# Reading moving tiles and writing banks from the last column to the first in a three-product float32 matmul

## The chip, the core and the metric

One Trainium2 chip, of which the kernel uses one core. TensorE multiplies a stationary tile of 128 x 128 by a moving tile of 128 partitions and up to 512 columns, and writes the output into one of eight banks of 512 float32 columns per partition. VectorE (DVE), ScalarE (ACT) and GpSimd (POOL) do the work between products; SyncE (SP) and GpSimd issue the transfers. The metric is the device time in microseconds of one execution; lower is better. The kernel before takes 2105.55 us, the median of 2 runs (2105.32 to 2105.77).

## The reference

One layer of a hybrid network over 512 latent tokens and 256 context tokens of 2048 features, all in float32:

- Modulation: `silu(cond) @ w_ada + b_ada` gives shifts, scales and gates, for the latent condition `c` and for the context condition `c_ctx`.
- Mixer: the normalised, modulated tokens go through `w_in` (2048 x 3072). A third is a Fourier part (a 2-D transform over tokens and 256 channels in each of four groups, then `w_fourier`), a third is the input of a recurrent part (a convolution of 4 taps, gates in 8 heads of 128, one scan forward and one backward, both seeded with the states of the context tokens), a third is its gelu gate. The two results are concatenated and go through `w_out` (2048 x 2048). The result is normalised, gated and added to `x`.
- Feed-forward: the normalised, modulated `x` goes through `w_up` (2048 x 11264), a convolution of 3 taps over tokens, `gelu(g) * v`, and `w_down` (5632 x 2048), and is again normalised, gated and added.

The output is the latent stream, 512 x 2048.

## The kernel before, in words

**Layout.** Features lie on the partitions, tokens on the columns: a tile of 128 features has 512 latent columns (`L`) or 256 context columns (`C`), so a token order is a column order. The 16 tiles of the normalised input are `h_hi` and `h_lo` (`hc_hi` and `hc_lo` for the context).

**Products of three.** Each float32 operand is split into a high part rounded to the format float32r (`_hi`, written by ScalarE) and the rest (`_lo`, written by VectorE as the difference). A product of two such operands is the sum of three float32r matmuls into the same bank: high by high, high weight by low moving tile, low weight by high moving tile. The helper `three` on TensorE issues them (lines 988, 989, 990), so nearly all matmuls of the kernel carry one of these three line numbers, whatever their stage. `start` clears the bank's sum at the first product, `stop` ends it at the last.

**Stages.** First the squares of `x` and of the context are summed over features by products with a matrix of ones (lines 998, 1001, 1027; the context's squares are written to `csq0` and half of `sq0`, two squares of 256 columns in each, by ScalarE at line 635). Then eight rounds of modulation: TensorE multiplies the two condition columns by strips of `w_ada` (line 1013), ScalarE copies the resulting rows from a bank to `ada_rows` (line 651, `copy_rows`), and TensorE turns them into columns by small products (line 1022, `turn`); the first input projections run between these rounds. Then come the other heads' projections and gates, the Fourier part, the output projection, and the feed-forward part in 11 chunks of 4 pairs of tiles. In each pair a part of the contraction is done by `seven_products`, with halves of 256 columns (`H`) in place of 512; `down` follows for the chunk before. The last chunk is finished in halves of 256 columns, and the residual is added at the end.

**Order of work.** Each engine has its own program, written out by hand. Weights come as a stream of units of 128 x 1024 float32 (512 KB), loaded by SP into a ring of slots (`w_raw`), rounded by ScalarE (line 602, `w_hi`) and split by VectorE (line 1532, `w_lo`). TensorE waits for `lo_done` once per unit, and its last product of a unit or of a bank raises the semaphore for whoever reads the bank or refills the slot. Banks are reused in turns.

**Plain products.** Sums over features or tokens use unsplit float32 operands; the compiler issues each as two instructions with the same columns. Line 1486 adds the residual this way through a moving tile made of two pieces of 256 columns (`x1_two`); lines 1468 to 1474 sum squares of 256 columns.

**Buffers.** `sq0`, `csq0`, `ss_x`, `ss_c`, `pos0`, `ada_rows` and the ring `ada0_raw` for the strips of `w_ada` stand one behind the other in a region that later stages use for other tiles.

**Falling column order before.** VectorE already walks some tiles from the last column to the first: the backward scans of the recurrent part (lines 1688 and 1691, beside the forward one in line 1685), the folding of tokens `n` and `512 - n` in the Fourier part (lines 1725 and 1726), and its unfolding (line 1771, whose sources are a tile and a bank, beside line 1769, which reads them forward).

Of the kernel before, what the change touches and what calls it, by code (L numbers as in the profile page):

```python
# [10 lines left out]
ACT = mybir.ActivationFunctionType  # L11
ds = bass.ds

P = 128
# [151 lines left out]
def build(nc, x1_d, x_t, ctx_t, par_d, late_d, stream, ada0, adabg, gates_d, tabs_d, wf_d, out_t):  # L166
    ctx = ExitStack()
    with ctx:
        def sem(name):
            return ctx.enter_context(nc.semaphore(name))  # L170

        def sbuf(stack, name, shape, dt=F32, side=None):
            return stack.enter_context(nc.sbuf_tensor(name, shape, dt, side=side))

        def twice(stack, raw, name, shape):

            with ExitStack() as s:
                first = sbuf(s, raw, shape)
            return first, sbuf(stack, name, shape, F32R)
# [34 lines left out]
        with ExitStack() as s:  # L214
            c0, hc_lo = twice(s, "c0", "hc_lo", [P, KT, C])
            hc_hi = sbuf(s, "hc_hi", [P, KT, C], F32R)
            with ExitStack() as s0:
                sq0 = sbuf(s0, "sq0", [P, 2, L])
                csq0 = sbuf(s0, "csq0", [P, 2, C])
                ss_x = sbuf(s0, "ss_x", [P, L])  # L220
                ss_c = sbuf(s0, "ss_c", [P, C])
                pos0 = sbuf(s0, "pos0", [P, NPOS])
                ada_rows = sbuf(s0, "ada_rows", [P, 2 * P])
                ada0_raw = sbuf(s0, "ada0_raw", [P, A0SLOTS, 1024])

        ada_raw12 = sbuf(mixer, "ada_raw12", [P, 2, ACOL], side="right")
# [137 lines left out]
        def rows_bank(c):  # L364

            return bank[5 + 2 * (c % 2)]
# [12 lines left out]
        a0_used, rows_copied, turned, mod_made = sem("a0_used"), sem("rows_copied"), sem("turned"), sem("mod_made")  # L379
# [209 lines left out]
        def _(act):  # L589
            chain = Chain(act, act_chain)  # L590
            a = nc.scalar
# [55 lines left out]
            def copy_rows(c):  # L647
                act.wait_ge(a0_used, A0UNITS * (c + 1))
                if c > 0:
                    act.wait_ge(turned, c)  # L650
                a.activation(ada_rows[:, :], rows_bank(c)[:, 0:2 * P], ACT.Copy).then_inc(rows_copied, 1)

            def round_h(c):
                for k in range(2 * c, 2 * c + 2):
# [6 lines left out]
            for c in range(NADA):  # L661
                copy_rows(c)
                round_h(c)
                hi(c + 1)
# [290 lines left out]
            c = NCH - 1  # L955
# [27 lines left out]
        def _(pe):  # L983
            t = nc.tensor

            def three(out, w, w_l, v, v_l, start, stop):

                t.matmul(out, w, v, start=start, stop=False)  # L988
                t.matmul(out, w, v_l, start=False, stop=False)  # L989
                return t.matmul(out, w_l, v, start=False, stop=stop)  # L990
# [54 lines left out]
            def gates_of_two(k):  # L1045

                for h in range(2):
                    mm = three(bank[UG_BANK[h]][:, :], *block_of(k // 2, 2 * h + k % 2), h_hi[:, k, :], h_lo[:, k, :],
                               k == 0, k == KT - 1)
                    if k == KT - 1:  # L1050
                        mm.then_inc(first_ug, 1)

            def inputs_of_two(k):

                for h in range(2):
                    bx, bc = ux_bank(h)
                    w, w_l = block_of(k // 2, 4 + 2 * h + k % 2)
                    three(bx[:, :], w, w_l, h_hi[:, k, :], h_lo[:, k, :], k == 0, k == KT - 1)
                    mm = three(bc[:, 0:C], w, w_l, hc_hi[:, k, :], hc_lo[:, k, :], k == 0, k == KT - 1)
                if k % 2:  # L1060
                    mm.then_inc(unit_used, 1)
# [381 lines left out]
            c = NCH - 1  # L1443
# [871 lines left out]
```

## Time and profile before

| | |
|---|---|
| Median of 2 runs | 2105.55 us |
| The profiled execution | 2105.41 us |
| Its span, first to last instruction | 2103.6 us |
| TensorE matmuls | 2071.2 us busy, 11682 instructions |
| TensorE weight loads | 1772.5 us |
| VectorE | 1529.6 us |
| ScalarE | 811.6 us |
| GpSimd | 78.7 us |
| DMA | 311.19 MB, mean 148 GB/s |
| Mean granted clock of TensorE | 0.996 |

Busy time is the time in which an engine has at least one instruction under way. Matmuls overlap in the pipeline: the duration of one is longer than the distance from its start to the next one's, so the pace of a series is read from the starts. `PE` is TensorE's matmuls, `PEld` its weight loads.

### The profile page before, as it was taken

Reading aid. Unit: us, or ns where it says so; the run is one execution under the profiler, and the core shown is the slowest. Engines: PE = TensorE matmul, PEld = TensorE weight load, DVE = VectorE, ACT = ScalarE, POOL = GpSimd, SP = SyncE. Lnnn points to the kernel's source line nnn. Section 1 sums busy time; section 2 is a strip of 40 time slices with the busy share of each in tenths; the row PEclk is TensorE's granted clock in tenths of the full one; section 3 lists DMA queues with packets and bytes.
Section 4 is the critical chain, followed back from the end, with each engine's and each line's share of the span. In section 5 each row is a group of like instructions: output and inputs, shape, how many; then the busy total and the mean of one; then the engine's idle time right before and its main releaser. Section 6 shows DMA issues by size and latency. Waiting matters only on the chain.

```text
span 2103.6 us, 28297 instructions
## 1 busy us (share of the span) xinstructions
PE 2071.2 (98%) x11682; PEld 1772.5 (84%) x11682; DVE 1529.6 (73%) x2202; ACT 811.6 (39%) x1077; POOL 78.7 (4%) x145
## 2 busy tenths in 40 slices
PE   7999999999999999999999999999999999999998
PEld 4678887888777888888889898898988889888887
DVE  5567978876988975867767676676766758577577
ACT  5346577543323442423324233332333424233243
POOL 0000000001110000000000000000000000000002
PEclk9999999999999999999999999999999999999999
DMA  9953424434876523333333333334233333232343
GB/s 394 408 204 110 154 96 161 137 109 173 323 277 225 181 90 134 100 128 111 110 130 101 138 103 103 129 101 140 100 120 121 100 130 100 91 101 101 100 172 109
DMA packets 86193, 311.19 MB, mean 148 GB/s; under 512 B 9456, under 2 KB 13552, under 8 KB 84016
## 3 DMA queue, kind: packets, MB, share of 16 engines
q1 hardware_dynamic: 67824, 243.09, 32.7%
q0 software_dynamic: 17424, 65.50, 9.1%
q8 instruction: 92, 1.51, 0.3%
q10 hardware_dynamic: 816, 0.79, 0.1%
q14 instruction: 37, 0.30, 0.0%
HBM read 300.95 MB, written 8.39 MB: 147 GB/s over the span
## 4 chain that ended last, share of the span: by engine, by line
PE 80%; DVE 2%; ACT 1%; DMA 1%; issue 0%; DVEq 0%; ACTq 0%
PE bank L988 26%; PE bank L990 26%; PE bank L989 26%; DMA w_raw<-in_stream 1%; PE bank L1099 1%; DVE acc L2167 0%; PE bank L1284 0%; DVE w_lo L1532 0%; ACT w_hi L602 0%; PE bank L1313 0%; PE bank L1194 0%; DVE acc L2139 0%; ACT lru_u L698 0%; DVE cv L1544 0%; DVE x L2193 0%
## 5 line engine op out<-in xcount | busy, mean ns | idle before, releaser
L988 PE MATMUL bank<-h_hi,w_hi 128*128 128x512 f32 (+1 forms) x1968 | 711.2, 361 | 4.2 <-ACT y_lru L671 1.2
L989 PE MATMUL bank<-h_lo,w_hi 128*128 128x512 f32 (+1 forms) x1968 | 708.6, 360 | 0.0
L990 PE MATMUL bank<-h_hi,w_lo 128*128 128x512 f32 (+1 forms) x1968 | 707.2, 359 | 0.0
L1532 DVE TENSOR_TENSOR w_lo<-w_raw,w_hi 128x1024 fp32r<-128x1024 f32 x260 | 316.0, 1222 | 157.9 <-ACT w_hi L602 157.8
L988 PEld LDWEIGHTS bank<-h_hi,w_hi 128*128 128x128 f32 x1968 | 372.3, 189 | 63.6 <-issue 11.9
L602 ACT ACTIVATE w_hi<-w_raw 128x1024 fp32r<-128x1024 f32 x260 | 273.0, 1056 | 389.1 <-DMA w_raw<-in_stream 389.0
L990 PEld LDWEIGHTS bank<-h_hi,w_lo 128*128 128x128 f32 x1968 | 372.1, 189 | 56.6
L989 PEld LDWEIGHTS bank<-h_lo,w_hi 128*128 128x128 f32 x1968 | 372.3, 189 | 49.0
L988 PE MATMUL bank<-act_hi,w_hi 128*128 128x512 f32 (+1 forms) x688 | 265.0, 385 | 1.7 <-DVE acc L2139 1.5
L990 PE MATMUL bank<-act_hi,w_lo 128*128 128x512 f32 (+1 forms) x688 | 264.2, 384 | 0.0
L989 PE MATMUL bank<-act_lo,w_hi 128*128 128x512 f32 (+1 forms) x688 | 264.2, 384 | 0.0
L598 ACT ACTIVATE w_hi<-w_raw 128x1024 fp32r<-128x1024 f32 x80 | 84.9, 1062 | 339.4 <-DVE w_raw L2040 339.4
L2067 DVE TENSOR_TENSOR acc<-acc,bank 128x512 f32<-128x512 f32 x144 | 98.3, 686 | 136.9 <-PE bank L990 136.9
L988 PEld LDWEIGHTS bank<-act_hi,w_hi 128*128 128x128 f32 x688 | 129.2, 188 | 27.9 <-DVE h_lo L1532 1.9
L989 PEld LDWEIGHTS bank<-act_lo,w_hi 128*128 128x128 f32 x688 | 129.3, 188 | 25.7
L990 PEld LDWEIGHTS bank<-act_hi,w_lo 128*128 128x128 f32 x688 | 129.3, 188 | 25.6
L1564 DVE SCALAR_TENSOR_TENSOR ada_acc<-ada_raw,csil,ada_acc 128x1024 f32<-128x1024 f32 x105 | 134.5, 1281 | 10.9 <-DMA ada_raw<-in_adabg 6.7
L550 POOL DMA_DIRECT2D ada_raw<-in_adabg x112 | 59.5, 532 | 1538.6 <-DVE ada_acc L1564 1139.1
L1528 DVE TENSOR_TENSOR w_lo<-w_raw,w_hi 128x1024 fp32r<-128x1024 f32 x80 | 97.5, 1219 | 0.0
L988 PE MATMUL bank<-t_hi,w_hi 128*128 128x256 f32 x320 | 90.6, 283 | 0.0
L989 PE MATMUL bank<-t_lo,w_hi 128*128 128x256 f32 x320 | 90.6, 283 | 0.0
L990 PE MATMUL bank<-t_hi,w_lo 128*128 128x256 f32 x320 | 90.5, 283 | 0.0
(340 smaller groups left out, 2711.4 us busy)
## 6 DMA issues: line engine op xcount, KB each, us to landing
w_raw<-in_stream SPq DMA_DIRECT2D x340, 512.0 KB, 3.5
ada_raw<-in_adabg POOLq DMA_DIRECT2D x112, 512.0 KB, 4.3
ada_raw<-in_ada SPq DMA_DIRECT2D x64, 512.0 KB, 13.5
x<-in_x_t SPq DMA_DIRECT2D x4, 1024.0 KB, 8.4
acc<-in_adabg SPq DMA_DIRECT2D x8, 512.0 KB, 6.1
x<-in_x_t POOLq DMA_DIRECT2D x4, 1024.0 KB, 9.4
x_kept_d<-x SPq DMA_DIRECT2D x4, 1024.0 KB, 5.6
c<-in_ctx_t SPq DMA_DIRECT2D x2, 1024.0 KB, 14.3
```

Of the source, the lines that this page charges most:

```text
L550: pool.dma_start(ada_raw(slot), adabg[COLS[q // KT] * KT + q % KT]).then_inc(ada_in[slot], 16)
L598: a.activation(hi_unit(n), raw_unit(n), ACT.Copy)
L602: a.activation(hi_unit(n), raw_unit(n), ACT.Copy).then_inc(hi_done, 1)
L988: t.matmul(out, w, v, start=start, stop=False)
L989: t.matmul(out, w, v_l, start=False, stop=False)
L990: return t.matmul(out, w_l, v, start=False, stop=stop)
L1099: mm = t.matmul(b[:, at + j:at + j + 1], ada_acc(n)[:, P * j:P * j + P], ones[:, 0:1], start=True, stop=True)
L1528: v.tensor_tensor(lo_unit(n), raw_unit(n), hi_unit(n).bitcast(F32), ALU.subtract)
L1532: v.tensor_tensor(lo_unit(n), raw_unit(n), hi_unit(n).bitcast(F32), ALU.subtract).then_inc(lo_done, 1)
L1564: v.scalar_tensor_tensor(dst, ada_raw(s), scale, dst, ALU.mult, ALU.add).then_inc(ada_eaten, 1)
L2067: v.tensor_tensor(tile(acc, m), tile(acc, m), bank[4 + m % 4][:, :], ALU.add).then_inc(down_added, 1)
```

## The change

The first thing in `three` is now to reverse the column order of its output and of both moving tiles. All three products thus read the moving tile from its last column to its first and write the output's columns from the last to the first; the weights stay as they are, and column j of the moving tile still goes to column j of the output. Products that do not go through `three` are untouched. Besides, `ada_rows` has no place of its own any more, and is the first half of `csq0`.

```diff
@@ -220,7 +220,7 @@
                 ss_x = sbuf(s0, "ss_x", [P, L])
                 ss_c = sbuf(s0, "ss_c", [P, C])
                 pos0 = sbuf(s0, "pos0", [P, NPOS])
-                ada_rows = sbuf(s0, "ada_rows", [P, 2 * P])
+                ada_rows = csq0[:, 0, :]
                 ada0_raw = sbuf(s0, "ada0_raw", [P, A0SLOTS, 1024])
@@ -648,7 +648,7 @@
                 act.wait_ge(a0_used, A0UNITS * (c + 1))
                 if c > 0:
                     act.wait_ge(turned, c)
-                a.activation(ada_rows[:, :], rows_bank(c)[:, 0:2 * P], ACT.Copy).then_inc(rows_copied, 1)
+                a.activation(ada_rows, rows_bank(c)[:, 0:2 * P], ACT.Copy).then_inc(rows_copied, 1)
@@ -985,6 +985,7 @@
             def three(out, w, w_l, v, v_l, start, stop):
 
+                out, v, v_l = out[:, ::-1], v[:, ::-1], v_l[:, ::-1]
                 t.matmul(out, w, v, start=start, stop=False)
                 t.matmul(out, w, v_l, start=False, stop=False)
                 return t.matmul(out, w_l, v, start=False, stop=stop)
```

## Rows read from the trace of the kernel before

**Rows 1.** The page: busy time, and TensorE's rows of 40 slices.

```profile
PE 2071.2 (98%) x11682; PEld 1772.5 (84%) x11682; DVE 1529.6 (73%) x2202; ACT 811.6 (39%) x1077; POOL 78.7 (4%) x145
...
PE   7999999999999999999999999999999999999998
...
PEclk9999999999999999999999999999999999999999
```

**Rows 2.** The page: the chain that ended last, by line.

```profile
PE bank L988 26%; PE bank L990 26%; PE bank L989 26%; DMA w_raw<-in_stream 1%; PE bank L1099 1%; DVE acc L2167 0%; PE bank L1284 0%; DVE w_lo L1532 0%; ACT w_hi L602 0%; PE bank L1313 0%; PE bank L1194 0%; DVE acc L2139 0%; ACT lru_u L698 0%; DVE cv L1544 0%; DVE x L2193 0%
```

**Rows 3.** Windows: busy time of each engine, clock, from 684 to 1500 us.

```profile
684.00:1500.00 816.00, 816.00 (x4520) 715.28 (x4519) 587.82 (x836) 281.29 (x342) 12.68 (x24) 1.00 0.35 119
```

**Rows 4.** Groups of line 988 by form: count, busy us, mean ns of one.

```profile
L988 PE MATMUL bank<-h_hi,w_hi 128*128 128x512 f32 x1408 | 552.9, 393 | 4.2 <-ACT y_lru L671 1.2 <-DVE hc_lo L1618 0.8 <-ACT sq L607 0.7
...
L988 PE MATMUL bank<-act_hi,w_hi 128*128 128x512 f32 x656 | 255.5, 390 | 0.1
...
L988 PE MATMUL bank<-h_hi,w_hi 128*128 128x256 f32 x560 | 158.3, 283 | 0.0
L988 PE MATMUL bank<-t_hi,w_hi 128*128 128x256 f32 x320 | 90.6, 283 | 0.0
...
L988 PE MATMUL bank<-t_hi,sums_hi 128*128 128x256 f32 x160 | 45.4, 284 | 0.0
...
L988 PE MATMUL bank<-hc_hi,w_hi 128*128 128x256 f32 x128 | 35.7, 279 | 0.0
...
L988 PE MATMUL bank<-h_hi,sums_hi 128*128 128x256 f32 x80 | 22.4, 280 | 0.0
...
L988 PE MATMUL bank<-act_hi,h_hi 128*128 128x256 f32 x64 | 18.2, 284 | 0.4 <-DVE acc L2139 0.4
...
L988 PE MATMUL bank<-xc_hi,g_hi 128*128 128x512 f32 x32 | 12.8, 400 | 3.5 <-issue 3.5
...
L988 PE MATMUL bank<-xc_hi,g_hi 128*128 128x256 f32 x32 | 9.0, 280 | 0.0
```

**Rows 5.** Timeline of TensorE: start us, us of one; a series' first and the next's.

```profile
1500.18 0.39 PE L988 MATMUL bank<-h_hi,w_hi 128*128 128x512 f32 x1
...
1509.70 0.28 PE L988 MATMUL bank<-h_hi,w_hi 128*128 128x256 f32 x1
...
1519.74 0.39 PE L988 MATMUL bank<-h_hi,w_hi 128*128 128x512 f32 x1
```

**Rows 6.** Timeline of TensorE: plain float32 products near the end.

```profile
2085.84 1.02 PE L1486 MATMUL bank<-late_raw,par 128*128 128x512 f32 x2
2086.69 0.59 PE L1468 MATMUL bank<-up_sum,par 128*128 128x256 f32 x2
2087.12 0.59 PE L1469 MATMUL bank<-up_sum,par 128*128 128x256 f32 x2
```

**Rows 7.** Groups of VectorE by form: forward and backward over columns.

```profile
L2036 DVE TENSOR_TENSOR sums_raw<-w_raw 128x256 f32<-128x256 f32 x40 | 16.7, 418 | 0.0
...
L1685 DVE TENSOR_TENSOR_SCAN lru_u<-lru_r,lru_i 128x768 f32<-128x768 f32 x8 | 14.1, 1758 | 0.3
...
L1691 DVE TENSOR_TENSOR_SCAN lru_u<-lru_r,lru_u,lru_i 128x512 f32<-128x512 f32 x8 | 10.3, 1285 | 0.3
...
L1688 DVE TENSOR_TENSOR_SCAN lru_u<-lru_r,lru_i 128x256 f32<-128x256 f32 x8 | 5.5, 691 | 0.3
...
L1769 DVE TENSOR_TENSOR y_four<-eo,bank 128x256 f32<-128x256 f32 x8 | 3.4, 422 | 0.3
...
L1726 DVE TENSOR_TENSOR eo<-y_four 128x255 f32<-128x255 f32 x8 | 3.3, 417 | 0.0
L1771 DVE TENSOR_TENSOR y_four<-eo,bank 128x255 f32<-128x255 f32 x8 | 3.3, 411 | 0.0
```

**Rows 8.** Timeline of ScalarE around the first copy of the rows.

```profile
29.38 0.85 ACT L635 ACTIVATE csq<-c 128x256 f32<-128x256 f32 x2 [0.91 <-PE bank L1027]
...
36.62 0.38 ACT L651 ACTIVATE ada_rows<-bank 128x256 f32<-128x256 f32 x1 [1.31 <-PE bank L1013]
```

## The prediction

> **What bounds the kernel now.** I read the page first, then the chain, then the groups, then single instructions. The busy table gives TensorE 2071.2 us of a span of 2103.6, and its row of forty slices stands at 9 but for the first and last; the granted clock is 9 or more tenths throughout, the higher of the two levels (2.4 GHz) [rows 1]. The chain of waits puts 26% of the span on each of lines 988, 989 and 990, the three products of `three`, and all else below 2% a line [rows 2]. In the long middle (684 to 1500 us) TensorE is busy 816.00 of 816.00 us while VectorE, next in line, has 587.82 [rows 3]. So nothing but TensorE sets the time there, and what happens to one product of `three` reaches the end almost undiminished.
>
> The size of that lever comes from counting. The groups by form [rows 4] show line 988 with 1408 + 656 + 32 = 2096 products of 512 columns and 560 + 320 + 160 + 128 + 80 + 64 + 5 x 32 = 1472 of 256 (32 of these 258); lines 989 and 990 repeat each count. That is 6288 long and 4416 short products. Their durations (393 and 283 ns) overlap, so the pace has to be read from start to start: 42 long ones from 1500.18 to 1509.70 us, 0.2267 us each; 84 short ones from 1509.70 to 1519.74, 0.1195 us each [rows 5]. 6288 x 0.2267 = 1425 us and 4416 x 0.1195 = 528 us: **1953 us**, 93% of the span, runs through the edited line. Doubling 256 columns adds 0.1072 us, 0.419 ns a column; what is left, 0.1195 - 0.1072 = 0.012 us, is a fixed part per product.
>
> **The change part by part.** *(a) The direction.* No instruction is added or removed: 10,704 products keep weights, sizes, order, bank and start and stop flags. Column j of the moving tile still goes to column j of the output, so only the order in time inside one product changes, and the finished bank is signalled by the same last product. No semaphore, DMA or queue moves; VectorE, ScalarE, SP and GpSimd see the same events. The only unknown is the price of a column when both address streams step by minus one element.
>
> No row of before has TensorE stepping backward, so I bound it. Above: the trace has the engine at a slower rate per column in its plain float32 instructions, 0.425 us for 512 columns (two instructions in 0.85 us, 2085.84 to 2086.69) and 0.215 for 256 (two in 0.43 us, 2086.69 to 2087.12) [rows 6]. At that rate the products cost 6288 x (0.425 - 0.2267) + 4416 x (0.215 - 0.1195) = 1247 + 422 = +1669 us. With the fixed 0.012 us kept on top of a doubled column price the additions are 0.2144 and 0.1072 us: 1348 + 473 = +1821 us. Below: at most the fixed part could vanish, 10,704 x 0.012 = -131 us.
>
> Between these ends I take 0, by the rows nearest in kind. VectorE already does this exact access elsewhere: line 1771 reads `cosine[:, C-1:0:-1]` in SBUF and `b[:, C-1:0:-1]` in a bank backward, 411 ns for 255 columns, beside 422 for 256 forward in line 1769; line 1726, one source of which runs backward in SBUF, takes 417 ns for 255, beside 418 for 256 forward in line 2036 [rows 7]. The memories thus give float32 columns in falling order at the same rate to that engine. Against leaning on it: VectorE takes one column in over 1 ns, TensorE in 0.42, so a path of its own that handles neighbours together could still trip. The reversed scans are mildly worrying: from 256 to 512 columns they add 1285 - 691 = 594 ns, 2.32 a column, where the whole forward scan of 768 takes 1758, 2.29 with its fixed part [rows 7]; at most some per cent. A gap in the moving tile is no burden either: line 1486 reads two separate runs of 256 at the 0.425 us that go into the slower rate above, but that rate may hide it [rows 6].
>
> The bank is where I see the risk. The Trainium skill ("PSUM — Partial Sum Buffer", Specifications) says that the bank's lines are 8 bytes, two float32 values, and that any non-contiguous pattern slows matmuls significantly. No row here shows TensorE writing a bank so. If a step of minus one counts as non-contiguous, the sum is the upper one above; if only leaving a line counts, falling pairs share lines as rising ones do, and the sum is 0.
>
> *(b) The shared buffer.* ScalarE's eight copies of 383 ns (line 651) now land in `csq0`'s first half. Its last squares are written by 29.38 + 0.85 = 30.23 us and summed before ScalarE can pass its wait for all 16 sums ahead of line 610; the first copy starts at 36.62, after an idle 1.31 us for TensorE's line 1013 [rows 8]. Program order already enforces this, no wait is added, and the 32 small products of line 1022 read 256 contiguous columns as before. The tile frees 1 KB per partition and moves only `ada0_raw`, whose 64 loads keep their waits. Cost 0; both ends: below 0 there is no wait to remove, above, even one copy fully exposed each time would be 8 x 0.383 = 3.1 us.
>
> **Sum.** 2105.41 (this profiled execution; 1.8 us outside its span) + 0 + 0 = 2105.4, and the median of the runs shown is 2105.55: **2105.5 us**, own range 2100 to 2112.
>
> **The rivals.**
> *Half rate (slower).* Place: every product of `three`, at the bank's write or the moving tile's read, where two neighbouring columns are taken together only when the address rises. It decides as soon as a column costs more than it does now: 2% of the time, 42 us, is 3.9 ns a product. Price +1669 to +1821 us: 3774 to 3926 us. For it: a column at 0.42 ns is faster than any other engine's, and 93% of the span has no slack [rows 3, 5]. Against it: rows 7. Chance 26%.
> *A turn at each product (slower).* The pipeline from one product into the next works only forward, and the fixed part doubles: +131 us, 2236 us. Forward, too, each product jumps back to the column where the one before began, and reversing keeps a jump of that length, which speaks against it. 6%. Slower than all these, with reading and writing each tripping: 3%.
> *The fixed part shrinks (faster).* If the 12 ns per product belong to the direction, up to -131 us, 1974 us. Plain instructions have only 2 x 0.215 - 0.425 = 0.005 us of it [rows 6], so it is not the engine's floor; but they repeat the same weights more often, which explains it better. 6%.
> *The edit does nothing:* the reversal of both sides could be folded away before the chip, with the same time; it lies inside the first case.
>
> **How the numbers follow.** No change 59%, half rate 26%, a turn 6%, beyond 3%, faster 6%. A measurement here tells about 2%, 42 us, from no change. Faster by over 2%: 0.06; within: 0.59; slower: 0.35. With no change alone at 59%, the range must take in the half rate too: 2100 to 3930 us, leaving out the faster case and the one beyond.
>
> **What would show it.** Right: long products start every 0.227 us and short ones every 0.120, 26% of the chain on each of the three lines, line 651 with the same 383 ns and waits. Half rate: 0.42 to 0.44 and 0.21 to 0.23 us, VectorE's busy share near 40% instead of 73%, ScalarE waiting on TensorE. A turn: both sizes later by the same ns, instead of in proportion to columns. The forecast fails if TensorE or its bank port takes falling addresses singly; the shared buffer fails if line 651 or 1022 shows a new releaser.

## The result: 1.6% slower, and the profile after

The changed kernel takes 2138.44 us (two runs, 2137.11 and 2139.77) against 2105.55 before: ratio 1.0156, 95% interval 1.0113 to 1.0200. That is 33 us more where the forecast had none, far from the 1670 to 1820 us of the half rate. It lies between the likeliest case's own range (to 2112 us) and the rivals, inside the wide range only because that reached to the half rate.

The page of the kernel after: busy times, TensorE's slices and granted clock, and the chain by line (the three products are now lines 989, 990 and 991).

```profile
PE 2108.4 (99%) x11682; PEld 1772.4 (83%) x11682; DVE 1530.2 (72%) x2202; ACT 810.9 (38%) x1077; POOL 78.6 (4%) x145
...
PE   7999999999999999999999999999999999999998
...
PEclk9999999999999999999999999999999999999999
...
PE bank L989 27%; PE bank L990 27%; PE bank L991 27%; DMA w_raw<-in_stream 1%; PE bank L1100 1%; DVE acc L2168 0%; PE bank L1309 0%; PE bank L1285 0%; PE bank L1195 0%; ACT w_hi L602 0%; DVE w_lo L1533 0%; PE bank L1314 0%; DVE acc L2140 0%; DVE cv L1545 0%; ACT lru_u L698 0%
```

Against [rows 1] TensorE gained 37.2 us of busy time with the same number of instructions; weight loads, VectorE, ScalarE and GpSimd moved by less than 1 us, and the clock still stands in the nines. The chain is the one of [rows 2]. The window of [rows 3], after:

```profile
684.00:1500.00 816.00, 815.46 (x4432) 698.40 (x4431) 578.95 (x823) 274.95 (x335) 12.68 (x24) 1.00 0.36 116
```

In the same 816 us TensorE gets through 4432 products where it did 4520, and waits for only half a microsecond (815.46 of 816.00 busy): 1.9% fewer in a stretch whose granted clock is 1.00 before and after. So each product got dearer. The timeline of TensorE after, where a series of long products and one of short ones begin (compare [rows 5]):

```profile
1525.15 0.40 PE L989 MATMUL bank<-h_hi,w_hi 128*128 128x512 f32 x1
...
1536.35 0.28 PE L989 MATMUL bank<-h_hi,w_hi 128*128 128x256 f32 x1
...
1546.28 0.40 PE L989 MATMUL bank<-h_hi,w_hi 128*128 128x512 f32 x1
```

48 long products in 11.20 us are 0.2333 us each (0.2267 before), 84 short ones in 9.93 us are 0.1182 (0.1195). The long ones lost 6.6 ns and the short ones gained 1.3. 6288 x 6.6 - 4416 x 1.3 = 41.5 - 5.7 = +35.8 us, where the two spans differ by 34.4: the paces of these two series explain the result within 1.4 us, and no wait does. They are a little larger than the average. Over all starts of the two traces, gaps of 300 ns and more left out, a long product goes from 227.4 to 233.4 ns and a short one from 120.6 to 119.5: 6288 x 6.0 - 4416 x 1.1 = 37.7 - 4.9 = +32.8 us.

The shared buffer did what was said of it. ScalarE's copies after, against [rows 8]:

```profile
L651 ACT ACTIVATE csq<-bank x8: 383/383/383, 36.9 to 117.8; 128x256 f32<-128x256 f32 x8
```

### The profile page after: what moved, and what is told of

Its sections match the earlier page's. It is cut to its first block, busy times and chain, and to the rows that moved or that the text cites. A ratio compares the mean times of both kernels' runs of the same rounds, so it can differ in the third digit from the quotient of the medians.

```text
span 2138.0 us, 28297 instructions
## 1 busy us (share of the span) xinstructions
PE 2108.4 (99%) x11682; PEld 1772.4 (83%) x11682; DVE 1530.2 (72%) x2202; ACT 810.9 (38%) x1077; POOL 78.6 (4%) x145
## 4 chain that ended last, share of the span: by engine, by line
PE 81%; DVE 1%; ACT 1%; DMA 1%; issue 0%; DVEq 0%
PE bank L989 27%; PE bank L990 27%; PE bank L991 27%; DMA w_raw<-in_stream 1%; PE bank L1100 1%; DVE acc L2168 0%; PE bank L1309 0%; PE bank L1285 0%; PE bank L1195 0%; ACT w_hi L602 0%; DVE w_lo L1533 0%; PE bank L1314 0%; DVE acc L2140 0%; DVE cv L1545 0%; ACT lru_u L698 0%
## 5 line engine op out<-in xcount | busy, mean ns | idle before, releaser
L989 PE MATMUL bank<-h_hi,w_hi 128*128 128x512 f32 (+1 forms) x1968 | 720.8, 366 | 3.0 <-ACT y_lru L671 1.1
L990 PE MATMUL bank<-h_lo,w_hi 128*128 128x512 f32 (+1 forms) x1968 | 719.4, 366 | 0.0
L991 PE MATMUL bank<-h_hi,w_lo 128*128 128x512 f32 (+1 forms) x1968 | 717.5, 365 | 0.0
L989 PE MATMUL bank<-act_hi,w_hi 128*128 128x512 f32 (+1 forms) x688 | 270.4, 393 | 1.5 <-DVE acc L2140 1.5
L991 PE MATMUL bank<-act_hi,w_lo 128*128 128x512 f32 (+1 forms) x688 | 269.7, 392 | 0.0
L990 PE MATMUL bank<-act_lo,w_hi 128*128 128x512 f32 (+1 forms) x688 | 269.7, 392 | 0.0
```

## The experiments

Theories at the start: the price sits in TensorE's read of the moving tile; in its write of the bank; in the shared buffer; or in traffic from other engines. Paces below are start to start of a whole series, divided by its count. In the separate kernels one row of the timeline is one series.

### e2, e3: the two edits apart

e2 adds only the reversal line to the kernel before; e3 changes only the buffer (and the copy in line 651 that writes it, left out here):

```diff
-                ada_rows = sbuf(s0, "ada_rows", [P, 2 * P])
+                ada_rows = csq0[:, 0, :]
```

> Only the reversal in the three products, the buffer of the rows left as before. The direction carries all: ratio 1.0156 to 1.0165, near 2139 us, long products every 0.233 us, short ones every 0.118. The shared buffer carries some: visibly less, below 1.010.

> Only the shared buffer, products forward. Theory of a free buffer: 1.000 within 0.002, 2105.5 us, line 651 at 383 ns with the same releaser. Rival, a cost by placement or order: anything over 1.002, up to the 33 us of the whole change.

Measured: e2 2137.25 us, ratio 1.0149 (1.0135 to 1.0163); e3 2106.71 us, ratio 1.0002 (0.9992 to 1.0013), line 651 at 383 ns. The direction carries all of it (a little less than the 1.0156 that I had expected at least), the buffer nothing that can be measured.

### e6, e7: reading backward and writing backward apart

```diff
+                v, v_l = v[:, ::-1], v_l[:, ::-1]        # e6
+                out = out[:, ::-1]                       # e7, instead
```

> Only the moving tiles are read backward, the output is written forward, so tokens come out in reverse order and the result is not the reference's; buffer as before. From the separate kernel (233.3 ns with read back at either direction of the write): the whole loss is here, ratio 1.014 to 1.017, long products 0.233 us. Rival, the write shares the loss inside the whole kernel: ratio below 1.010.

> Only the output is written backward, moving tiles are read forward; tokens come out in reverse order, so the result is not the reference's; buffer as before. From the separate kernel (227.5 ns against 226.7): no loss, ratio 0.998 to 1.003, long products 0.227 us, short ones 0.1195. The rival of the prediction's risk at the bank: up to 1.015.

Measured: e6 2137.26 us, ratio 1.0148 (1.0133 to 1.0164); e7 2106.00 us, ratio 0.9998 (0.9989 to 1.0008). The timeline of e7 keeps the paces of before, 48 long products in 10.90 us (0.2271) and 84 short ones in 10.04 us (0.1195):

```profile
1520.44 0.39 PE L989 MATMUL bank<-h_hi,w_hi 128*128 128x512 f32 x1
...
1531.34 0.28 PE L989 MATMUL bank<-h_hi,w_hi 128*128 128x256 f32 x1
...
1541.38 0.39 PE L989 MATMUL bank<-h_hi,w_hi 128*128 128x512 f32 x1
```

The bank, which I had called the risk, takes falling columns for nothing that can be measured: reading backward alone costs what the whole reversal costs, writing backward alone nothing. All of the loss is in the read.

### e4, e8: short and long products apart

```diff
+                if out.shape[-1] < L:                    # e4; e8: == L
+                    out, v, v_l = out[:, ::-1], v[:, ::-1], v_l[:, ::-1]
```

> Only products of fewer than 512 columns are reversed (4416 of 10704), buffer as before. By the paces of the two traces these gain some 1.0 to 1.2 ns each: 4.4 to 5.3 us faster, ratio 0.9975 to 0.9979, and the loss of the whole change sits in the 6288 long ones (6.6 ns each, 41.5 us). Rival: the reversal costs something at every product and the short ones' nearer starts are given back in waits: 1.000 or above.

> Only the 6288 products of 512 columns are reversed, both sides, buffer as before. Sum of the whole change less what the short ones gave: 1.0149 + 0.0031 = 1.018, 2144 us; long products 0.233 us, short ones 0.1195. Rival, the parts do not add (the gain of the short ones came only with less time elsewhere): 1.015 or below.

Measured: e4 2099.32 us, ratio 0.9969 (0.9956 to 0.9981), faster than the kernel before; e8 2148.21 us, ratio 1.0197 (1.0182 to 1.0212). e8's excess of 42 us is near the 6288 x 6.6 ns = 41.5 of its term; e4's gain of 7 us is a little above the 5.7 of its own and the 5.3 that I had expected at most. e8's ratio lies just above its expected 1.018, which had been made from e2's 1.0149 and e4's measured gain of 0.0031; the 0.0017 between is within what the three intervals leave open. Both signs are clear of the noise, and the whole change is their difference.

### e1, e5: TensorE alone

No edit: separate kernels that load once, then issue series of products like this one.

```python
for i in range(24):  # 512 read back, write back
    mm = t.matmul(bank[2][0:128, 511::-1], w[:, 128 * (i % 16):128 * (i % 16) + 128], v[:, i % 4, 511::-1], ...)
```

> A separate kernel that computes none of the reference: after one load it issues series of 24 products (float32r unless said), TensorE alone at work, with moving tile and output each forward or backward, 512, 384, 256 or 128 columns, and some with narrower or repeated weights. Theory P (the price is one per column, on TensorE itself): a backward product costs 0.4557 ns a column and no fixed part, a forward one 0.4167 a column and 13.3 ns; so 512: 226.7 forward, 233.3 backward; 384: 173.3 and 175.0; 256: 120.0 and 116.7; 128: both held at 112 to 120 by the weight load. Theory F (a fixed price of a long product, as a boundary that only 512 columns cross): 384 backward 160 to 166 or 180, not 175. Rival O (other engines' traffic makes the difference in the whole kernel): alone, backward and forward are equal within 1 ns at every size. Theory R (the moving tile's read): read back, write forward has the backward pace. Theory W (the bank's write): read forward, write back has it. If the weight load disturbs the read, weights of 32 columns bring forward and backward together near 216 ns.

The timeline of e1: start, time of the series, line. Lines 65, 67, 69, 71 are 512 columns with read and write forward; both backward; read backward only; write backward only. Lines 81, 83 are 256 columns forward and both backward. Lines 113, 115 are the same at 512 columns in bfloat16.

```profile
28.51 5.60 PE L65 MATMUL bank<-v,w 128*128 128x512 f32 x24
33.95 5.77 PE L67 MATMUL bank<-v,w 128*128 128x512 f32 x24
39.55 5.76 PE L69 MATMUL bank<-v,w 128*128 128x512 f32 x24
45.15 5.62 PE L71 MATMUL bank<-v,w 128*128 128x512 f32 x24
50.61 4.35 PE L73 MATMUL bank<-v,w 128*128 128x384 f32 x24
...
67.49 3.03 PE L81 MATMUL bank<-v,w 128*128 128x256 f32 x24
70.36 3.01 PE L83 MATMUL bank<-v,w 128*128 128x256 f32 x24
73.20 3.00 PE L85 MATMUL bank<-v,w 128*128 128x256 f32 x24
...
133.94 5.36 PE L113 MATMUL bank<-vb,wb 128*128 128x512 bf16 x24
139.13 5.34 PE L115 MATMUL bank<-vb,wb 128*128 128x512 bf16 x24
144.31 5.34 PE L117 MATMUL bank<-vb,wb 128*128 128x512 bf16 x24
```

From each start to the next, over 24: 226.7, 233.3, 233.3 and 227.5 ns at 512 columns; 119.6 and 118.3 at 256; 216 and 216 in bfloat16. The effect is whole with TensorE alone, so rival O (other engines) falls, theory R stands and W falls. bfloat16 has neither the loss nor the extra 11 ns that even the forward float32r product carries. Theory P had 512 right, whose paces it was made from, and 384 forward nearly (174.2); backward, 384 columns took 177.9 ns, between P's 175.0 and F's 180, and neither came. Weights of 32 columns gave 229.6 forward and 233.3 backward, not 216: a shorter weight load does not remove the loss. It takes nearly half of the forward advantage away instead, for which e9 offers a possible reason below.

> The second separate kernel, none of the reference: series of 24 float32r products, TensorE alone, of 64 to 512 columns forward and backward with weights of 32 columns (so that the weight load limits nothing) and of 192 to 480 with weights of 128; then 512 columns in other orders: the two halves swapped but forward within; groups of eight and of four, last group first, forward within; groups of four and of 32 in rising order, backward within; halves backward within; even then odd columns; 256 columns from column 2, 4 and 8; 512 with another bank each time. Theory G (the loss grows with the length of an unbroken falling run): 227 forward and 233 backward at 512, crossing near 300 columns, and halves backward within near twice the 118 ns of 256 columns (237) or, if the run and not the instruction counts, below 233. Theory L (a lost step at every line or group boundary crossed downward): groups of four, last first, cost as much as backward (233) or more, and groups backward within but rising cost no more than forward (227). Rival (a fixed price of a falling start address at the next product's beginning): all patterns that begin at the last column cost 233, all others 227.

In e5, backward products with weights of 32 columns take 31.7, 60.0, 89.2, 117.9, 146.7, 175.4, 204.6 and 233.3 ns at 64 to 512 columns in steps of 64: a straight line of 0.450 ns a column, 7% over the 0.419 of the prediction. But forward, with the same weights, the same lengths take 32.5, 59.6, 88.3, 116.7, 146.7, 173.3, 203.8 and 230.8 ns, nearly the same line, so the 0.450 is not a price of the direction. With weights of 128 columns backward costs nothing at 320 columns (146.7 ns against 147.1 forward), 2.1 ns more at 352 and 4.6 more at 416: the loss does not grow evenly with the length. The orders at 512 columns, in the timeline of e5 (line 125 halves swapped, forward within; 127 eights and 129 fours, last group first, forward within; 131 rising fours, backward within; 133 rising groups of 32 and 135 halves, backward within; 137 even, then odd columns):

```profile
130.18 5.64 PE L125 MATMUL bank<-v,w 128*128 128x512 f32 x24
135.66 5.77 PE L127 MATMUL bank<-v,w 128*128 128x512 f32 x24
141.26 5.76 PE L129 MATMUL bank<-v,w 128*128 128x512 f32 x24
146.86 5.62 PE L131 MATMUL bank<-v,w 128*128 128x512 f32 x24
152.32 5.77 PE L133 MATMUL bank<-v,w 128*128 128x512 f32 x24
157.92 5.76 PE L135 MATMUL bank<-v,w 128*128 128x512 f32 x24
163.52 11.04 PE L137 MATMUL bank<-v,w 128*128 128x512 f32 x24
174.38 2.98 PE L139 MATMUL bank<-v,w 128*128 128x256 f32 x24
```

228.3, 233.3, 233.3, 227.5, 233.3, 233.3 and 452.5 ns. None of the three theories fits. G fails at the halves, L at the groups of 32, the rival at the eights, whose first column is not the last one. What the two cheap rows share is that at every moment the read stands within four columns of where a forward read would stand (in line 125, but for a whole half). A step of two columns in the moving tile doubles the time. One more odd thing came up: 256 columns forward started at column 4 took 113.3 ns instead of 119.6.

### e9, e10: where the tiles lie

That last number pointed away from direction, to the place of the tiles. The series of e9 and e10 start the moving tile, or the weights, some columns further on, `o` or `ow` in this form:

```python
mm = t.matmul(bank[1][0:128, 0:512], w[:, ds(128 * (i % 16) + ow, 128)], v[:, ds(L * (i % 4) + o, 512)], ...)
```

> The third separate kernel, none of the reference: series of 48 float32r products, TensorE alone, of 512 and 256 columns, forward, whose moving tile starts 0 to 32 columns into its tile, or whose weights start 4 to 64 columns in; a few backward, and a few with one moving and one weight tile throughout. The last run had 256 forward from column 4 at 113.3 ns, from columns 0, 2 and 8 at 119.6, 117.5 and 117.1. Theory S (the start of the moving tile within a group of 4 or more columns sets the forward loss): 512 from column 4 also gains some 6 ns or more (below 221), the rest keeps 224 to 227; backward moves by as much. Theory C (the forward extra of 11 ns over the bfloat16 pace comes from the weight load reading beside the moving tile, by their relative place): moving the weights by 4 columns changes the pace as moving the other tile does, and moving both cancels. Rival (a counting artefact at the edges of short series): with 48 products all starts agree within 1 ns.

> The fourth separate kernel, none of the reference: series of 24 float32r products, TensorE alone, of 512 and 256 columns, with the moving tile starting 0 to 60 columns (steps of 4), 64 and 128 columns behind a place that lies at the same offset modulo 256 bytes as the weights; with the weights moved by 8 to 112 columns instead; backward with starts 0 to 56; and both moved together. Theory C (what counts is the distance of the two tiles modulo 64 columns, 256 bytes): 512 forward is 226.7 ns at starts 0, 64 and 128 alone and 232 to 233 at all others; both moved together keep 226.7; for 256 columns the moving tile from column 48 repeats the 113.3 ns that weights from column 16 gave; backward is 233 at every start because it never keeps the distance. Rival (backward has its own loss on top of the distance): backward stays above every forward start, over 234 somewhere, or forward at odd distances falls below 230.

In e9 the plain start gives 226.7 ns, but columns 2, 4, 6, 8, 12, 16 and 32 give 231.9 to 233.3, forward; weights from column 32 give 232.5 and from column 64 again 226.7. Theory S falls, and so does the counting artefact at 512 columns. Theory C had that moving both tiles cancels; with one tile of each throughout, both from column 4, the product took 230.0 ns, half of the way. Weights of 32 columns, one behind the other, are at an equal place and 32 columns off in turn; the mean of 226.7 and 232.5 is 229.6, which is what e1 had. (Weights of 64 columns, always at an equal place, took 230.4 forward in e1, so this reason is not shown.) The timeline of e10: lines 62, 64, 66 are 512 columns forward from column 0, 4, 8; 90, 92, 94 and 96 from column 56, 60, 64 and 128; 98 has the weights moved by 8; 108 is backward from column 0; 124 and 126 have both tiles moved by 16 and by 32.

```profile
28.46 5.60 PE L62 MATMUL bank<-v,w 128*128 128x512 f32 x24
33.90 5.72 PE L64 MATMUL bank<-v,w 128*128 128x512 f32 x24
39.45 5.77 PE L66 MATMUL bank<-v,w 128*128 128x512 f32 x24
...
106.47 5.75 PE L90 MATMUL bank<-v,w 128*128 128x512 f32 x24
112.06 5.61 PE L92 MATMUL bank<-v,w 128*128 128x512 f32 x24
117.50 5.64 PE L94 MATMUL bank<-v,w 128*128 128x512 f32 x24
122.98 5.61 PE L96 MATMUL bank<-v,w 128*128 128x512 f32 x24
128.43 5.75 PE L98 MATMUL bank<-v,w 128*128 128x512 f32 x24
...
156.22 5.76 PE L108 MATMUL bank<-v,w 128*128 128x512 f32 x24
...
201.04 5.65 PE L124 MATMUL bank<-v,w 128*128 128x512 f32 x24
206.52 5.65 PE L126 MATMUL bank<-v,w 128*128 128x512 f32 x24
```

Forward from 0, 60, 64 and 128: 226.7 to 228.3 ns. From 16: 229.6, as with the weights moved by 48 (228.8) or 112 (229.2). From the other starts of the scan: 230.8 to 234.6. Weights moved by 8: 232.9. Both moved together: 228.3 and 228.7. All eight backward starts: 233.3 to 233.8. What is above 226.7 at an equal offset is the beginning of a series: the first ten products or so of the series from 64 and of the two with both tiles moved take up to 236 ns each. Their last twelve average 226.7 or 226.8 ns from start to start, as do those of every other series of e9, e10 and e13 with neither tile moved, one moved by 64 or 128 columns, or both moved by 16 or 32.

So at 512 columns theory C holds in the main: moving either tile alone costs, moving it by 64 columns or both by 16 or 32 does not. But the distance modulo 64 columns is not the whole rule. The moving tile from column 60 is as cheap as from 0 (226.7), while weights from column 4, the same distance, took 233.3 in e9; both from column 4 took 230.0; and the moving tile from column 16 took 233.3 in e9 and 229.6 in e10. A sign of e10's rival, that backward has a loss of its own, came too: forward fell below 230 at 16 and 60. Against it, backward from the seven unequal starts costs no more than from column 0, so the two losses do not add. At 256 columns the distance says little: forward takes 113 to 120 ns, lowest in e10 at starts 28 and 48, but weights moved by 16 gave 113.3 in e9 and 117.9 in e10, and the moving tile from column 4 gave 113.3 in e5, 116.9 in e9 and 119.2 in e10.

This case's kernel has its tiles at equal offsets. By the sizes of the buffers that lie between them, before and after, `h_hi`, `h_lo`, `hc_hi`, `hc_lo`, `t_hi`, `t_lo`, `act_hi`, `act_lo`, `w_hi` and `w_lo` all begin at the same offset modulo 256 bytes.

### e11: only the weights moved, nothing backward

```diff
+        sbuf(ctx, "shift", [P, 8])
         w_raw, w_lo = twice(ctx, "w_raw", "w_lo", [P, RING, UNIT])
         w_hi = sbuf(ctx, "w_hi", [P, RING, UNIT], F32R)
+        sbuf(ctx, "shift_back", [P, 56])
```

> The kernel before, all products forward, with the ring of weights (w_raw, w_lo, w_hi) 8 columns, 32 bytes, further on, so that its tiles are no longer at the same offset modulo 256 bytes as the moving tiles; everything behind the ring stays at its offset modulo 256 (with the shared buffer, which makes the room). Nothing is read backward. Theory C (a falling order costs only because it gives up the equal offset): the long products go to 233 ns and the short ones to about 118, and the kernel to 2136 to 2145 us, ratio 1.014 to 1.019, as with the reversal. Rival (the falling order itself costs): 2106 us, ratio 1.000, long products 0.227 us.

Measured: 2137.50 us, ratio 1.0152 (1.0134 to 1.0169), where the reversal alone gave 1.0149. The timeline of e11:

```profile
1518.11 0.39 PE L990 MATMUL bank<-h_hi,w_hi 128*128 128x512 f32 x1
...
1529.31 0.28 PE L990 MATMUL bank<-h_hi,w_hi 128*128 128x256 f32 x1
...
1539.24 0.39 PE L990 MATMUL bank<-h_hi,w_hi 128*128 128x512 f32 x1
```

48 long products in 11.20 us (0.2333), 84 short ones in 9.93 us (0.1182): to the last digit the paces of the reversed kernel, with every tile read forward. So the relative place of the two tiles sets the pace in the whole kernel too, and giving up the equal offset is enough for the whole loss. That the reversal loses by the same mechanism is likely from this (the same paces for long and for short products, and losses that do not add in e10), but not shown: no kernel was run with the weights moved and the tiles read backward.

### e13: is there a start at which backward is cheap?

> The fifth separate kernel, none of the reference: series of 24 float32r products of 512 columns, TensorE alone, backward with the moving tile starting at every odd column from 1 to 63 and at 2, 10, ... 58, and forward at columns 1, 2, 3, 61, 62 and 63. So far backward was 233 ns at the eight starts 0, 8, ... 56. Theory C1 (backward can be cheap too, at a narrow distance that steps of 8 columns missed, as forward is cheap only within some 4 columns of an equal offset): one or two neighbouring starts give 227 to 229 ns. Theory C2 (the cheap pace needs both streams to keep their distance from column to column or to walk a way that a falling moving tile never does): 233 ns at every start, while forward has a rise from 227 to 231 or more between columns 0 and 4 and the same on the other side.

Forward from column 0 took 226.7 ns. The 32 odd starts and the 8 even ones between those of e10 took 233.3 to 242.1 backward. Together with e10's, none of 48 backward starts comes below 233.3: C2's number. Forward, the starts 1, 2, 3, 61, 62 and 63 took 237.5, 232.9, 230.4, 238.3, 234.6 and 230.0, so the cheap place is narrow, and columns 1 and 61 are dearer than any start at a multiple of four. Backward above 234 (28 of e13's 40 backward starts, the dearest 242.1 from column 31) was the other sign of e10's rival, so an added loss of the falling order is not excluded at such starts.

### e12: a version faster than both

```diff
-            def three(out, w, w_l, v, v_l, start, stop):
+            def three(out, w, w_l, v, v_l, start, stop, back=True):
+                if back and out.shape[-1] < L:
+                    out, v, v_l = out[:, ::-1], v[:, ::-1], v_l[:, ::-1]
...
+        sbuf(fin, "t_shift", [P, 48])
         t_raw, t_lo = twice(fin, "t_raw", "t_lo", [P, 4, 3 * H])
         t_hi = sbuf(fin, "t_hi", [P, 4, 3 * H], F32R)
+        sbuf(fin, "t_shift_back", [P, 16])
...
-        sbuf(fin, "gap_to_x1", [P, 256])
+        sbuf(fin, "gap_to_x1", [P, 192])
...
-                    product(alone_v[:, 0:H], block_of(n, 6 + ab), t4, False, False)
+                    product(alone_v[:, 0:H], block_of(n, 6 + ab), t4, False, False, False)
...
```

The two other products with a tile of `t_hi` and `t_lo` get `False` for `back` in the same way.

> A version that should beat both: long products forward as before; the short ones whose moving tile is t_hi or t_lo (1440 of 4416) forward, but with those two tiles 48 columns further on (a distance of 48 modulo 64 columns, where the separate kernel had 113 ns for 256 columns); the other short ones backward; rows in csq0, which makes the room. Theory C, with the separate kernel's paces: against the kernel before 1440 x 6 ns = 8.6 us less for the moved tiles and, as in the run with the short products backward, some 1 ns for each of the other 2976, 3 us: 2094 to 2096 us, ratio 0.994 to 0.995. Rival (the low pace at that distance needs a whole series of the same distance; between neighbours at another distance it is lost): the moved tiles stay near 118 ns and the kernel at 2099 us, ratio 0.997, as with the short products backward alone.

Measured: 2099.81 us, ratio 0.9969 (0.9957 to 0.9982), the same as e4: the rival's number came. In the timeline of e12 84 short products still take 9.93 us, and six of them in a row with the moved tiles 0.70 us, where the same six, read backward, take 0.71 in e4 (1509.72 to 1510.43 us):

```profile
1505.98 0.28 PE L992 MATMUL bank<-h_hi,w_hi 128*128 128x256 f32 x1
...
1509.18 0.28 PE L992 MATMUL bank<-t_hi,w_hi 128*128 128x256 f32 x1
...
1509.88 0.29 PE L992 MATMUL bank<-h_hi,w_hi 128*128 128x256 f32 x1
...
1515.91 0.39 PE L992 MATMUL bank<-h_hi,w_hi 128*128 128x512 f32 x1
```

Moving the two tiles bought nothing beyond reversing all short products. Why the 113 ns did not come is open: the rival had put it down to neighbours at another distance, but the separate kernels do not repeat that pace for one start either. e4 is the simpler of the two and beats both kernels, by 0.3% against the one before.

## Why the prediction was wrong, point by point

- **What bounds the kernel** held. TensorE sets the time, 10,704 products pass through the edited line, and a change of pace reaches the end undiminished: +35.8 us by the paces, +34.4 in the span.
- **(a) The direction: this is the step that failed.** The bounds, -131 and +1821 us, held; between them I took 0, because VectorE's backward rows cost no more [rows 7]. I had noted that its column takes over twice TensorE's and that "a path of its own" could trip, but gave that only the price of a whole half rate and, as a turn, of a doubled fixed part. The term measured +33 us: in the series shown 6.6 ns for each long product and -1.3 for each short one. A cost of a few ns a product was never among the cases, though 3.9 ns was worked out as the point from which it matters. The wide range held the result only by reaching to the half rate, which is luck. VectorE's rows could hardly have shown it: by e11 the pace of TensorE hangs on the relative place of the two tiles that it reads, for which VectorE's rows have no counterpart.
- **The fixed part** was misread. The 12 ns per product [rows 5] were taken as a cost of going from one product to the next, perhaps of changing weights. With one weight tile throughout the product still took 227.1 ns (e1), while bfloat16 needed 216. Most of it belongs to float32r, and moves with the tiles' place: at the prediction's 0.419 ns a column (0.2144 and 0.1072 us) a long product has 12.3 ns of it forward and 18.9 backward, a short one 12.3 and 11.0. (The -131 us of the prediction is 10,704 times the unrounded 12.3 ns; the 0.012 printed there gives 128.) That is also why a turn at each product (same ns for both sizes) and a shrinking fixed part (a gain for both) each describe half of what happened, and neither the whole.
- **The bank.** The risk was put at the bank's write. By e7 it costs nothing, 0.9998 (0.9989 to 1.0008). The rule of the Trainium skill ("PSUM — Partial Sum Buffer", Specifications) that any non-contiguous pattern slows matmuls does not take in a step of minus one; my other reading of it, that falling pairs share an 8-byte line, agrees with the time, though no run shows that this is the reason. A step of two in the output was not tried.
- **(b) The shared buffer** at 0 was right: 1.0002 (0.9992 to 1.0013).
- **The mechanism, as far as it is shown.** With weights of 128 columns, a float32r product of 512 columns read forward takes 227 ns when its moving tile lies at the same offset modulo 256 bytes as its weights (230 with both tiles from column 4), and 229 to 238 at the other starts tried but one, column 60; read backward it takes 233 to 242 at all 48 starts. e11 breaks the equal offset alone and the reversal the rising order alone; each costs 1.5%. That the price of the reversal is in the read of the moving tile is shown (e6, e7, e1); that it is the price of the lost offset is argued. The Trainium skill ("TensorE: Matmul & The Clock Gate", Step-by-step: what each phase is for) says that the two reads have independent ports, so that loading weights takes nothing from the moving tile. The measurement does not fit two reads that leave each other alone: moving only the weights by 32 bytes made the long products 6.6 ns slower.
- **What stays open:** what collides inside. Weights of a quarter of the width took the same 233.3 ns backward, so it is not simply the number of weight columns; and why backward is never cheap while groups of four read backward are, no run settles. Nor do the runs say why short products gain from the reversal, why one start can have two paces in two runs, or what the low 113 ns of 256 columns hangs on.

## What to carry to other kernels

Before a tile's order, start or buffer is changed in a kernel bound by TensorE with float32r operands, note where its two tiles lie modulo 256 bytes, and read the pace from start to start before and after: 3% per product showed in no wait, in TensorE's share of the span only as 99% for 98%, and in the mean duration of a long product as 400 ns for 393. Evidence that one engine takes an access for nothing does not carry over to another: here VectorE's backward rows cost no more and TensorE's did. When an edit's price is unknown, put a small cost per item between nothing and the disaster: here 6.6 ns in 227 made the whole result.

## What the runs showed of the hardware that I had not expected

- float32r at 512 columns with weights of 128, one after the other, forward: 226.7 ns at equal offsets once a series has settled (230.0 with both tiles from column 4), up to 234.6 elsewhere in steps of four columns, 237.5 from column 1 and 238.3 from column 61. bfloat16: 216, read either way.
- Moving only the weights by 32 bytes costs a whole kernel 1.5% (e11).
- Read backward with weights of 32 columns, products of 64 to 512 columns take 0.450 ns a column, and forward almost as much; with weights of 128, 512 columns backward take no less than 233.3 ns at any of 48 starts. Backward writing costs nothing that can be measured (0.9998, 0.9989 to 1.0008).
- A moving tile read with a step of two float32r columns takes twice as long, 452.5 ns for 512.
- Short products (256 columns) range from 113.3 to 120.0 ns; at equal offsets forward 119.6 to 120.0, otherwise mostly less, by no rule that the runs show. Reversing them alone made the kernel 0.3% faster (e4).
